# Multiplying the identity into an unread PSUM bank at TensorE's waits in the norms

## What is computed

```python
def rms_norm(x, g):
    xf = x.astype(jnp.float32)
    y = xf * lax.rsqrt(jnp.mean(xf * xf, axis=-1, keepdims=True) + NORM_EPS)
    return (y * g.astype(jnp.float32)).astype(x.dtype)
...
    for i in range(DEPTH):
        h = modulate(rms_norm(x, norm_g[i, 0]), sh1, sc1)
        y = nsa_mixer(...) if i % N_MIXERS == 0 else swa_sink_mixer(...)
        x = x + (1 + g1)[:, None, :] * rms_norm(y, norm_g[i, 1])
        h = modulate(rms_norm(x, norm_g[i, 2]), sh2, sc2)
        y = squared_relu_mlp(h, mlp_w_up[i], mlp_w_down[i])
        x = x + (1 + g2)[:, None, :] * rms_norm(y, norm_g[i, 3])
...
        h = rms_norm_2(x, norm_mix_w[l])
        x = x + hybrid_mixer(h, ...)
        h = rms_norm_2(x, norm_xattn_w[l])
        m = rms_norm_2(mem, norm_mem_w[l])
        x = x + memory_cross_attention(h, m, ...)
        h = rms_norm_2(x, norm_ffn_w[l])
        x = x + conv_ffn(h, ...)
    return rms_norm_2(x, norm_final_w)
```

## Time and profile before

| | us |
|---|---|
| median of 3 runs | 2279.24 |
| lowest and highest | 2276.93, 2283.43 |
| profiled execution, its own time | 2277.44 |
| its span, first to last instruction | 2275.6 |
| TensorE busy within the span | 2027.9 (89%) |
| VectorE, ScalarE, GpSimd busy | 1150.0, 692.6, 905.4 |
| mean granted TensorE clock | 0.937 |

### The profile page before, as it was taken

One profiled execution on the slowest core, in us unless ns is written; L12 is line 12 of the kernel. 1 busy time (PEld: TensorE's weight loads), 2 busy tenths in 40 slices (PEclk: granted clock), 3 DMA queues, 4 the chain that ended last, 5 costly groups with the idle time before them and its releaser, 6 DMA issues.

```text
span 2275.6 us, 26750 instructions
## 1 busy us (share of the span) xinstructions
PE 2027.9 (89%) x10200; PEld 1644.5 (72%) x10200; DVE 1150.0 (51%) x1681; ACT 692.6 (30%) x1199; POOL 905.4 (40%) x513
## 2 busy tenths in 40 slices
PE   2988999799999979797999998895889698999997
PEld 1778777578888857675888886684768366888886
DVE  6575776674564655536342443374332325626354
ACT  2343554332222232533222223223223223222222
POOL 1355554245445414642444443230236023444442
PEclk9998999799999979897999999896899698999999
DMA  7546332345555314411333322120134012323331
GB/s 260 188 170 189 108 94 105 117 164 178 194 172 194 126 48 160 139 62 47 98 97 94 101 93 92 57 74 27 38 121 130 28 47 74 101 93 94 99 95 65
DMA packets 78375, 252.15 MB, mean 111 GB/s; under 512 B 10680, under 2 KB 11192, under 8 KB 77880
## 3 DMA queue, kind: packets, MB, share of 16 engines
q1 hardware_dynamic: 78264, 250.61, 33.5%
HBM read 235.21 MB, written 15.37 MB: 110 GB/s over the span
## 4 chain that ended last, share of the span: by engine, by line
issue 44%; PE 27%; POOL 18%; DVE 4%; DMA 3%; ACT 1%; SPq 1%; POOLq 0%; DVEq 0%; ACTq 0%
POOL wl L723 17%; PE ps L783 6%; PE ps L785 6%; PE ps L784 6%; PE ps L995 2%; PE ps L938 2%; PE ps L967 1%; DMA qscr<-rot_l 1%; DMA qscr<-rot_ls 1%; PE ps L1215 1%; POOL pr L744 1%; DMA raw<-in_units 1%; PE ps L1192 1%; ACT pr L2056 1%; DVE st L1476 1%
## 5 line engine op out<-in xcount | busy, mean ns | idle before, releaser
L723 POOL TENSOR_TENSOR wl<-raw,wh 128x1024 fp32r<-128x1024 f32 x309 | 761.8, 2468 | 1249.9 <-ACT wh L1934 1249.9
L1934 ACT CAST wh<-raw 128x1024 fp32r<-128x1024 f32 x309 | 323.8, 1051 | 1151.0 <-PE ps L785 1039.4
L783 PE MATMUL ps<-ah,wh 128*128 128x512 f32 x1512 | 602.6, 399 | 29.7 <-DVE al L1305 17.9
L784 PE MATMUL ps<-ah,wl 128*128 128x512 f32 x1512 | 594.2, 393 | 0.0
L785 PE MATMUL ps<-al,wh 128*128 128x512 f32 x1512 | 594.1, 393 | 0.0
L783 PEld LDWEIGHTS ps<-ah,wh 128*128 128x128 f32 x1512 | 286.8, 190 | 107.6 <-issue 21.7
L785 PEld LDWEIGHTS ps<-al,wh 128*128 128x128 f32 x1512 | 287.3, 190 | 60.8
L784 PEld LDWEIGHTS ps<-ah,wl 128*128 128x128 f32 x1512 | 288.1, 191 | 57.6 <-issue 0.7
L783 PE MATMUL ps<-hh,wh 128*128 128x512 f32 x688 | 268.5, 390 | 3.9 <-DVE hl L1891 3.9
L785 PE MATMUL ps<-hl,wh 128*128 128x512 f32 x688 | 267.7, 389 | 0.0
L784 PE MATMUL ps<-hh,wl 128*128 128x512 f32 x688 | 267.7, 389 | 0.0
(11 more groups left out here) (284 smaller groups left out, 2373.2 us busy)
## 6 DMA issues: line engine op xcount, KB each, us to landing
raw<-in_units SPq DMA_DIRECT2D x309, 512.0 KB, 3.5
ada_mlp<-in_ada SPq DMA_DIRECT2D x64, 512.0 KB, 3.6
ada<-in_ada SPq DMA_DIRECT2D x16, 512.0 KB, 5.3
qs<-qscr SPq DMA_DIRECT2D x32, 256.0 KB, 3.9
ada_in<-in_ada SPq DMA_DIRECT2D x16, 512.0 KB, 3.5
ks<-kscr SPq DMA_DIRECT2D x24, 256.0 KB, 4.8
x<-in_xT SPq DMA_DIRECT2D x1, 2048.0 KB, 13.3
qscr<-rot_h SPq DMA_DIRECT2D x8, 256.0 KB
```

Of the source, the lines that this page charges most:

```text
L723: nc.gpsimd.tensor_tensor(wl[:, slot], raw[:, slot], wh[:, slot].bitcast(F32), ALU.subtract).then_inc(lo_done, 1)
L783: nc.tensor.matmul(out_ap, wh[:, slot, k], high[:, k0 + k], start=first and k == 0, stop=False)
L784: nc.tensor.matmul(out_ap, wl[:, slot, k], high[:, k0 + k], start=False, stop=False)
L1934: a.copy(wh[:, slot], raw[:, slot]).then_inc(hi_done, 1)
```

## The change

A helper `keep_busy(count)` issues `count` matmuls with the identity as both operands: 128x128 weights and 512 moving columns (the identity four times over), fp32r, into bank 7, which nothing reads there. TensorE's queue gets them ahead of these waits:

- 2 ahead of the wait for `sq_added` and 2 ahead of that for `sq_made` in `gemm_squared` (7 calls each),
- 5 at the head of `root_spread` (13 calls),
- 2 ahead of each `square_sum`, save in the very first norm (5 times 8),
- 7 at the head of each `gemm` that is called with `ready=(a_ready, n)` and n above 0: 15 calls. Seven of them stand behind a norm, eight are the later up blocks (three in each MLP, two in the FFN).

That is 28 + 65 + 80 + 105 = 278 matmuls. Nothing else is changed.

```diff
         def gemm(first, count, high, low, turned=False, tokens=S, ks=DC, ready=None):
 
+            if ready is not None and ready[0] is a_ready and ready[1]:
+                keep_busy(7)
             n0 = done[0] - first
...
+        def keep_busy(count):
+
+            for _ in range(count):
+                nc.tensor.matmul(ps[:, 7].rearrange("p (a b) -> p a b", a=4), ident_r[:],
+                                 ident_r[:][:, None, :].to_broadcast([P, 4, P]), start=True, stop=True)
+
         def root_spread(slot, tokens=S):
+            keep_busy(5)
             pe.wait_ge(inv_made, squares[0])
...
             q = squares[0]
+            if q:
+                keep_busy(2)
             pe.wait_ge(sq_made, DC * q + c + 1)
...
             q = squares[0]
+            keep_busy(2)
             pe.wait_ge(sq_added, 6 * (gemms_squared[0] + 1))
             quarters(4 + q % 2, sqs, True, False)
+            keep_busy(2)
             pe.wait_ge(sq_made, DC * (q + 1))
```

## The result

The changed kernel takes 2294.34 us (median of 4 runs, 2294.09 to 2294.82) against 2279.12 for the kernel before (2276.93 to 2283.43): a ratio of 1.007, 95% interval 1.0056 to 1.0084, or 15.2 us more. The profiled execution took 2294.82 us, its span is 2293.0, and the mean granted clock, as a share of full speed, rose from 0.937 to 0.955. So the clock was helped and the time got longer.

A forecast was written before the change was run, and what follows sets the result against it. It took TensorE to bound dense products, and to wait for VectorE and ScalarE in the norms. 12.7 + 1.3 + 0.6 - 4.4 - 3.4 + 0.5 - 0.3 = +7.0 us on the median gave 2286 us, range 2279 to 2294.

The forecast's parts named there:

- part 3: Pairs on the path at four second `quarters` and the memory tokens' squares: 1.3 and 0.6 us, +1.9 together.
- part 2: Fills in waits of the norms: free at full clock; at the lower clock 0.02 us per pair, 0.49 per five.
- Part 1: Eight later up blocks, where TensorE waits for nothing: seven fills each paid in full at 0.227 us, +12.7 us.
- Part 4: Faster clock in norms: first spreads -4.4 us, second spreads -3.4 in three of four, +0.5 in the fourth, memory unit -0.3.
- (a): Rival: the squares' stretch stays at the lower clock in all four norms; +12.5 us, 2292; chance 0.22.
- (b): Rival: clock in all norms runs as before, fills there at half speed; +19 us, 2298; chance 0.08.
- (d): Rival: identity matmuls run faster than products, as weights stay the same; at half the pace +0.7 us, 2280; chance 0.05.

The follow-up runs named there:

- e1: Changed kernel without the seven fills ahead of each of the eight later up blocks: 2282.78 us, 1.0014 times the kernel before.
- e2: Kernel before plus only the seven fills ahead of each of the eight later up blocks: 2293.87 us, ratio 1.0068.
- e11: Changed kernel with only the pair ahead of the first `quarters` of `gemm_squared` and the fives ahead of spreads: 2280.79 us, 1.001 times the kernel before.
- e5: Changed kernel with one identity matmul instead of two ahead of each square of `square_sums`: 2290.66 us, one execution.
- e9: Changed kernel with two sets of four small fp32 matmuls of the kind of `quarters` instead of each pair in `square_sums`: 2289.41 us, one execution.
- e4: Kernel before run once more, nothing edited, for a second trace: 2281.1 us, one execution.
- e8: Changed kernel with four fp32 matmuls, 128x128 weights and 128 moving columns, instead of each fp32r pair in `square_sums`: 2300.1 us, one execution.
- e10: e3 without the pairs ahead of squares 1 to 6, the nine ahead of the first square kept: 2276.51 us, 0.9996 times the kernel before.
- e3: Changed kernel with fills only in waits longer than they are, none ahead of later up blocks: 2266.78 us, 0.9949 times the kernel before.
- e7: Changed kernel with weights of 32 columns instead of 128 in the fp32r pairs of `square_sums`: 2282.58 us, one execution.

## Why the prediction was wrong

The direction was right and the largest term exact; the time, 2294.34, fell just outside the range (2279 to 2294), and the change is twice the 7 us that I forecast. The step that failed is the price of a pair next to `quarters` (part 3, and part 2 at the lower clock): I took 0.45 us for it, and the runs show 0.78 between two `quarters` (1.02 against 0.24).

**Part 1, the later up blocks, right.** 8 times 1.59 us; e1 and e2 show it from both sides. In the trace of the changed kernel too the starts lie 0.227 us apart, for the identity (seven from 543.10 to 544.68) as for products.

**Part 2, "covers a wait", wrong at the lower clock.** I took a pair and `quarters` to need 1.28 us of a round of 1.26. It needs 1.74 (828.38 to 830.12): four rounds of 1.63 to 1.74 in the norm behind MLP 0 are why its second spread comes 11.80 us behind the first of its squares (828.38 to 840.18) and not 10.35 as before (824.67 to 835.02), where I had 0.02 for each. For a five I took 2.13 us, and in e11 the spread starts 2.30 behind it.

**Part 3, "lie on the path", the step that failed most.** I priced a pair at its starts, 2 times 0.227, and took `quarters` to follow at once. In its place stands 0.35 + 0.66 us for `quarters`, pair, `quarters`, against 0.24 for two `quarters` in a row. Of that, 0.45 is the pair and 0.24 the `quarters`; the remaining 0.3 are the two changes of kind, which e5 shows by taking one matmul away (a round of 0.77), and e9 by making all of one kind (0.66). For the memory tokens I had halved `quarters` to 0.12 us as well. But their rounds take 1.01, no less than the 1.02 of four matmuls, and the round of e9 is 0.66 and not 0.60, three sets at 0.22: a set of two takes as long as one of four. The four second `quarters` cost 2.6 us instead of 1.3 and the memory tokens' squares 3.8 instead of 0.6: 4.5 us of the miss.

The rows ahead of the prediction had a hint. The records of products in a row overlap by 0.16 us, and I used that overlap everywhere; no row before showed `quarters` next to another kind without a wait between them, so it was to be bounded from both sides, and the upper bound, that the next starts at the modelled end, is within 0.07 us of what happened.

**Part 4, the clock, right in its mechanism.** First spreads: -4.4, as forecast, and -4.9 against the second trace of the kernel before (e4); that all of them ran fast was in part luck, since in e1 and e8 one each was slow behind the same fills. Second spreads: all four at 1.16 us, one more than I took, and the gap ahead of the squares dropped the clock in three of four, to 0.50 (in two by the first square, in one from the second on). But the last two squares come 0.66 us apart and their round takes 1.02, which costs 0.4 in each norm, and the slow rounds of part 2 cost more: -1.6 instead of -2.9. Rivals (a) and (b) did not come about. Neither did (d).

**What no part had.** In the last FFN block TensorE waits 2.2 us for a low part. It did so before as well, but there the clock held (first two rows, 1.00 for 2232 to 2235), and here it falls for the products behind (last two, 0.53 for 2248 to 2251):

```profile
2232.01 0.50 PE L783 MATMUL ps<-hh,wh 128*128 128x512 f32 x1 [2.24 <-DVE hl L1891]
2232.36 0.40 PE L784 MATMUL ps<-hh,wl 128*128 128x512 f32 x1
```

```profile
2247.94 0.63 PE L783 MATMUL ps<-hh,wh 128*128 128x512 f32 x1 [2.23 <-DVE hl L1904]
2248.37 0.63 PE L784 MATMUL ps<-hh,wl 128*128 128x512 f32 x1
```

Eight products at 0.43 instead of 0.23 us are the 1.6 us. Nine of the 13 traces have this fall: all with fills in the norms except e10, and none of the three without them (both of the kernel before, and e2). So it goes with the fills, though in e1, e3 and e11 none stands within 330 us ahead of it. How they bring it about no run shows.

With the mis-sized terms set right the sum is 7.0 + 4.5 + 1.3 - 0.3 = 12.5 us; with the last FFN block 14.1, within the interval of the measurement (12.8 to 19.1). The rest of the 17.4 between the two traces is the banded attention's 2.6 and 0.8 elsewhere, stretches that scatter over the traces of this study with no cause shown.

## What to carry to other kernels

In these runs a filler matmul was free only where the wait it fills is longer than the filler, the change of kind on both of its sides counted, and at the lower clock as well: a pair where nothing waits put the second `quarters` back by 0.59 us, and at the lower clock it made rounds of 1.26 us into 1.74. Put it by the gap (e3 wins 11.6 us with 237 fills, of which its trace shows 8.5 at the norms; the change loses 15.2 with 278). Look at every call of the helper that carries the fill: here eight of 15 calls had nothing to wait for and cost 12.7 us, more than the 8.5 of e3 at the norms. What a fast clock gave back was small where products are paced by another engine (a chunk of `al` every 1.44 us): the gain lay in the few small matmuls that others wait for, such as a spread of 1.16 us instead of 2.08.

## What the runs showed of the hardware

- Small fp32 matmuls with weights of 32 columns start about 0.07 us ahead of the modelled end of a matmul of another kind (another width in e8, another type and moving length in e7, all three in the changed kernel), and the next of another kind the same behind them; two sets of four of one kind start 0.24 us apart (2262.97 and 2263.21 in the earlier trace rows). Between a spread (fp32, 128 columns) and an identity matmul (fp32r, 128 columns) no such wait shows: in the changed kernel the fill at 432.81 starts 0.24 us ahead of the spread's end at 433.05, and in e11, at the lower clock, the spread at 436.26 starts 0.20 us ahead of the fill's end at 436.46. Products with weights of 128 columns, other ones each time, follow each other at 0.227 us from start to start, 0.16 us ahead of the modelled end. Why only changes of kind with narrow weights pay is open.
- The clock fell behind a single wait of 2.23 us in nine traces (0.53 in the changed kernel) and held at 1.00 in four (the last FFN block). The cross attention has a long and a short course, 75.9 us at a mean clock of 0.69 in the kernel before and 70.8 at 0.76 in e3, with the same instructions (the stretch, before and then e3):

```profile
1763.60:1839.50 75.90, 52.47 (x128) 27.74 (x129) 25.70 (x78) 15.40 (x50) 4.77 (x3) 0.69 0.07 21
```

```profile
1758.30:1829.10 70.80, 47.14 (x129) 25.39 (x129) 25.62 (x78) 15.47 (x50) 4.81 (x3) 0.76 0.08 23
```

  From the second unit of the memory tokens' products to the cross attention's last product it is 158.7 to 159.0 us in e3, e5 and e7, 162.2 in e10 and 163.3 to 164.4 in the other nine, the changed kernel among them. What chooses it was not settled; it can move a single trace of e3 by 5 us, while its ratio rests on six runs.
